# A two-layer hybrid decoder step on one core: another first stage, and a regrouping of function tables, splits and masks on the other engines

## The chip, the core and the metric

The kernel runs on one core of one Trainium2 chip, as one program. The metric is the device time of a run in microseconds; where several runs are given, it is their median. The core's engines are TensorE (PE in the rows), VectorE (DVE), ScalarE (ACT), GpSimd (POOL) and the queue of SyncE (SP); they run at the same time and meet at semaphores. PEld is TensorE's weight load, PEq the sequencer of TensorE.

## The reference

`reference.py` computes one inference step of two layers for a prompt of 512 tokens and eight samples of eight tokens each (576 tokens in all), at a model width of 1024. Layer 0 has Mamba-2 heads and sparse-attention heads in parallel, layer 1 gated DeltaNet heads and dilated sliding-window heads; each layer ends in a squared-ReLU MLP of width 4096, with a root-mean-square norm before and after mixer and MLP. The work starts with

```python
y = x * rsqrt(mean(x * x) + eps) * norm_w
```

for all 576 tokens, and the inputs of the convolutions and of the mixers' step sizes are products of this y.

## The kernel before

Tokens are kept turned: 128 partitions hold 128 of the 1024 channels, one tile for each k from 0 to 7 (KT = 8), with the 576 tokens (TOK) in the free dimension. Every f32 product is made from rounded parts: `HH` is the high part of the activations (fp32r), `HTr` the low part, and of each weight chunk ScalarE writes the high part (`split_high`, L283, the CAST in the rows) and GpSimd the low part (`split_low`, L295); then high x high, high x low and low x high are three matmuls of 288 columns. Chunks of weights are 1 MB and come through a ring of buffers that SyncE's queue fills (`fill_ring`).

The program is a list of stages. Each stage is a block: all engines meet at its end (`L114`), so a stage lasts until its last engine is done. Inside a stage each engine runs its instructions in the order in which they are written; nothing is scheduled by a planner. `split_high(K, act, n)` and `split_low` send all chunks up to n that have not been sent yet, so where they are called decides in which stage and behind what the work is done.

The stages that the change touches, in order of time: `initialise` (GpSimd makes iotas, VectorE the identity and the masks, the queue starts x, two transfers, and the first weights); `first_norm` (TensorE turns x: for each k five transposes, L362; VectorE and ScalarE copy them out by turns, ScalarE squares 128 x 576 per k, L393, VectorE adds the eight squares, L420; a product with ones sums over the partitions, L367; Ln and Exp give the root, L396 and L398; VectorE multiplies, L427, ScalarE rounds, L401, VectorE subtracts, L431; TensorE makes the products for dt and for sconv's first chunk); the SSM convolution (`project_conv`, units u of 128 channels; its products of gates, L904); `ssm_norm`; the compression of sparse attention; `layer_tail`, once a layer (norms with Ln and Exp at L2313 to L2327, the output and MLP products L2407, L446, L2518 and L2420); `gdn_scalars` (gates of the delta rule, and `LevelMasks`, 30 integer operations of VectorE); two `project_conv` stages for the delta rule, each with `roots`, which normalise q and k, L927 and L931; two times two `gdn_pair` stages, each for two heads a and b, whose steps go by counted semaphores (L3236: identity minus the level-0 matrix; L3239 and L3240: k times beta and k times decay); and after each two pairs `gdn_norm`, whose end is

```python
            for i in range(N):
                act.activation(RS[:, i, :], RS[:, i, :], ACT.Exp, scale=-0.5).then_inc(rs_ready, 1)
            split_high(K, act, chunk + 1)
```

The CAST of the next chunk stands behind the norm's functions on ScalarE, and `split_low(K, pool, chunk + 1)` is all that GpSimd has in that stage.
## Time and profile before

| what | value |
|---|---|
| median of 3 runs | 2828.17 us (2827.36 to 2830.39) |
| time of the profiled execution | 2830.34 us |
| span in its trace, first to last instruction | 2827.7 us |
| mean granted clock of TensorE | 0.948 of full speed |
| instructions | 44348 |
| TensorE busy | 2577.0 us, 91% of the span |
| VectorE, ScalarE, GpSimd busy | 1253.7, 966.6, 910.6 us |

The profiled execution took 2.6 us more than its span, and 2.2 us more than the median. All durations below are from it. A row of a timeline is the start, the duration, the engine, the line, the operation, what it writes and reads, and in brackets the idle time before it and what ended it.

### The profile page before, as it was taken

How to read it: one execution, taken by the hardware profiler on the slowest of the kernel's cores; microseconds unless marked ns; L12 is line 12 of the kernel's file. 1: busy time of each engine (PE TensorE's matmuls, PEld its weight loads, DVE VectorE, ACT ScalarE, POOL GpSimd, SP SyncE). 2: the span in 40 equal slices, each digit the busy share in tenths (PEclk: the TensorE clock that was granted, in tenths of full speed). 3: DMA queues.
4: the chain of work that ended last, by engine and by line, in shares of the span. 5: the costliest groups of instructions: out<-in, count | busy, mean ns of one | idle time of the engine just before them, and what ended most of it. 6: DMA issues, size and time to landing. Idle time of an engine off the chain costs nothing. (4 is left out here: it accounts for less than half of the span.)

```text
span 2827.7 us, 44348 instructions
## 1 busy us (share of the span) xinstructions
PE 2577.0 (91%) x18431; PEld 2302.5 (81%) x18431; DVE 1253.7 (44%) x2509; ACT 966.6 (34%) x1743; POOL 910.6 (32%) x449
## 2 busy tenths in 40 slices
PE   7889899987989999989988898889998887999997
PEld 5856796556979999978977797778776687999997
DVE  6785303776152223364644365432126444422225
ACT  4442222663252112152632353231225434221212
POOL 2351230332353333342344234423320015433331
PEclk9989998998999999989998899889999998999999
DMA  5212465330312222222211121112330532222221
GB/s 157 92 40 87 83 134 180 157 161 1 90 60 75 90 75 90 75 79 81 75 33 32 32 75 33 32 32 81 108 116 6 173 116 68 76 89 81 84 88 51
DMA packets 206677, 232.74 MB, mean 82 GB/s; under 512 B 40460, under 2 KB 165228, under 8 KB 205870
## 3 DMA queue, kind: packets, MB, share of 16 engines
q1 hardware_dynamic: 204398, 229.66, 26.0%
...
q10 hardware_dynamic: 2080, 0.25, 0.1%
...
## 5 line engine op out<-in xcount | busy, mean ns | idle before, releaser
L295 POOL TENSOR_TENSOR WRr<-WR,WH 128x2048 fp32r<-128x2048 f32 (+2 forms) x100 | 440.7, 4407 | 1040.9 <-ACT WH L283 949.1
L2407 PE MATMUL PS<-HHr,WRr 128*128 128x288 f32 x1104 | 327.0, 296 | 0.0
L283 ACT CAST WH<-WR 128x2048 fp32r<-128x2048 f32 (+2 forms) x100 | 182.2, 1823 | 355.1 <-DMA WR<-in_mlp_w 140.8
L446 PE MATMUL PS<-YTr,WRr 128*128 128x288 f32 x1024 | 303.5, 296 | 0.0
L446 PE MATMUL PS<-HHr,WH 128*128 128x288 f32 (+1 forms) x896 | 271.9, 303 | 22.4 <-PEq L114 21.0
L446 PE MATMUL PS<-YTr,lt_WX 128*128 128x288 f32 x1408 | 282.1, 295 | 0.0
L446 PE MATMUL PS<-HTr,WH 128*128 128x288 f32 (+1 forms) x896 | 268.8, 300 | 0.0
L446 PE MATMUL PS<-HHr,WRr 128*128 128x288 f32 (+1 forms) x896 | 268.6, 300 | 0.0
L295 POOL TENSOR_TENSOR WRr<-WR,lt_WX 128x2048 fp32r<-128x2048 f32 x34 | 157.9, 4645 | 256.4 <-ACT lt_WX L283 256.4
L2407 PE MATMUL PS<-HHr,WH 128*128 128x288 f32 x800 | 237.5, 297 | 0.3 <-POOL WRr L295 0.3
L2407 PE MATMUL PS<-HTr,WH 128*128 128x288 f32 x800 | 237.0, 296 | 0.0
L446 PEld LDWEIGHTS PS<-YTr,lt_WX 128*128 128x128 f32 x1408 | 227.3, 188 | 0.1
L2407 PEld LDWEIGHTS PS<-HHr,WRr 128*128 128x128 f32 x1104 | 209.1, 189 | 0.0
L446 PEld LDWEIGHTS PS<-YTr,WRr 128*128 128x128 f32 x1024 | 192.1, 188 | 0.0
L446 PEld LDWEIGHTS PS<-HHr,WH 128*128 128x128 f32 (+1 forms) x896 | 171.7, 192 | 24.6 <-POOL WRr L295 16.4
L2819 DVE TENSOR_TENSOR YT<-YT 128x576 f32<-128x576 f32 x64 | 55.0, 860 | 276.6 <-ACT YT L2711 265.9
L446 PEld LDWEIGHTS PS<-HTr,WH 128*128 128x128 f32 (+1 forms) x896 | 171.7, 192 | 0.6
L446 PEld LDWEIGHTS PS<-HHr,WRr 128*128 128x128 f32 (+1 forms) x896 | 171.4, 191 | 0.6
L476 PE MATMUL PS<-WH,HHr 128*128 128x512 f32 (+2 forms) x400 | 154.8, 387 | 6.1 <-PEq L114 6.1
L476 PE MATMUL PS<-WRr,HHr 128*128 128x512 f32 (+3 forms) x400 | 152.9, 382 | 0.0
L2711 ACT ACTIVATE YT<-PS 128x576 f32<-128x576 f32 x56 | 36.5, 652 | 340.3 <-PE PS L2407 340.3
L2407 PEld LDWEIGHTS PS<-HHr,WH 128*128 128x128 f32 x800 | 151.3, 189 | 0.7 <-POOL WRr L295 0.6
...
## 6 DMA issues: line engine op xcount, KB each, us to landing
...
```

Source lines behind the costliest of these rows:

```text
L283: act.copy(high_slot(K, i, used), K.WR[:, n % RING, 0:used]).then_inc(K.hi, 1)
L295: pool.tensor_tensor(K.WRr[:, n % RING, 0:used], K.WR[:, n % RING, 0:used], high_slot(K, i, used).bitcast(F32), ALU.subtract).then_inc(K.l ...
L446: last = pe.matmul(out, a, b, start=(n == 0), stop=(n == 3 * len(terms) - 1))
L476: last = pe.matmul(K.PS[0:a.shape[1], bank, 0:n], a, w[:, k, :], start=(half == 0 and k == 0 and m == 0), stop=(half == 1 and k == kt - 1 ...
L2407: last = pe.matmul(out, a[:, k, c], h[:, k, x], start=(n == 0), stop=(n == 3 * KT - 1))
L2711: act.activation(in_halves(whole(r, j)), both_halves(K, u % 2), ACT.Relu).then_inc(relu_done, 1)
L2819: dve.tensor_tensor(x, x, x, ALU.mult).then_inc(sq_done, 1)
```

## The change

The stage `initialise` is dissolved into `first_norm`. x comes in five transfers, one per tile of 128 tokens; TensorE turns a tile as it lands; ScalarE sums the squares of each tile token by token, with the accumulator, so the root is one number per partition; a diagonal matrix of the roots (`DG_`) is the moving operand of a second product of x, which comes out turned and scaled in one; ScalarE multiplies by the norm's weight and rounds to `HHr`, VectorE makes `HTr` in one operation. The dt products stand between the scaled ones, the sconv products behind them all. The masks are made between the copies of tiles.

Beside that: `logs_and_exps` puts one table set that has both Ln and Exp in front of the norms, `roots` and both layer tails, and four further stages load a named set at their start; with it the program has 33 table loads, before 62. In the SSM convolution the products and functions of the gates' sums stand two units later. `LevelMasks` moves from `gdn_scalars` into the first `project_conv` of the delta rule, four operations a unit. The split of chunk + 2 in `gdn_scalars` stands ahead of a wait. In `gdn_pair` the order of VectorE's L3236 and L3239/L3240 changes, and the last pair takes over the split of chunk + 1, which `gdn_norm` had.

```diff
+def logs_and_exps(act):
+    act.preload_act_table_set("natural_log_exp_and_others")
...
+                for t, n in TILES:
+                    src = K.x_prompt[0][t * P:(t + 1) * P, :] if t < NT else K.x_sample.rearrange("b s d -> (b s) d")
+                    sp.dma_start(XS[0:n, t, :], src).then_inc(K.x_tile[t], 16)
+                fill_ring(K, sp, RING - 1)
...
+                logs_and_exps(act)
+                act.wait_ge(x_zero, 3)
+                for t, n in TILES:
+                    act.wait_ge(K.x_tile[t], 16)
+                    if t:
+                        act.wait_ge(sq_done, t)
+                    act.activation(SQ[0:n, :], XS[0:n, t, :], ACT.Square, accum_out=ss[0:n, t:t + 1]).then_inc(sq_done, 1)
+                inv_rms(act, K, ss[:], D, sq_done, TT, rs_link).then_inc(rs_done, 1)
+                act.wait_ge(rs_done, 1)
+                act.wait_ge(ident_in, 1)
+                for t in range(TT):
+                    act.mul(DG_[:, t, :], K.ident[:], ss[:, t:t + 1]).then_inc(diagonal, 1)
+                split_high(K, act, K.at["dt"])
+                act.wait_ge(small_out, 1)
+                for k in range(KT):
+                    act.wait_ge(h_mm, k + 1)
+                    act.mul(K.HH[:, k, 0:TOK], scaled_x(k), K.normT[:, 0, k:k + 1]).then_inc(hi_done, 1)
+                    if k == 2:
+                        split_high(K, act, K.at["sconv"])
...
+                pe.wait_ge(x_copied, TT)
                 for k in range(KT):
-                    if k % 2:
-                        act.wait_ge(turned, k + 1)
-                        act.copy(K.XT[:, k, 0:TOK], K.PSF[:, (k % 3) * 1024:(k % 3) * 1024 + TOK]).then_inc(x_act, 1)
-                    x_copied(act, k)
                     if k >= 2:
-                        act.wait_ge(added, k - 1)
-                    act.activation(SQ[:, k % 2, :], K.XT[:, k, 0:TOK], ACT.Square).then_inc(sq_done, 1)
-                split_high(K, act, K.at["sconv"])
-                act.wait_ge(summed, 1)
-                act.activation(in_halves(RS[:]), K.PS[:, 6:8, 0:HALF], ACT.Ln, scale=1.0 / D, bias=K.eps[:]).then_inc(rs_link, 1)
-                act.wait_ge(rs_link, 1)
-                act.activation(RS[:], RS[:], ACT.Exp, scale=-0.5).then_inc(rs_done, 1)
+                        pe.wait_ge(hi_done, k - 1)
+                        pe.wait_ge(lo_done, k - 1)
+                    for t, n in TILES:
+                        if k == 0:
+                            pe.wait_ge(diagonal, t + 1)
+                        last = pe.matmul(scaled_x(k)[:, t * P:t * P + n], XS[0:n, t, k * P:(k + 1) * P], DG_[0:n, t, 0:n],
+                                         start=True, stop=True)
+                    last.then_inc(h_mm, 1)
...
+                    if k == 1:
+                        dt_w = split_wait(K, pe, K.at["dt"])
+                        pe.wait_ge(small_out, 2)
+                    if k >= 1:
+                        dense(k - 1, dt_w, SH, 6)
+                dense(KT - 1, dt_w, SH, 6).then_inc(K.mm, 1)
+                conv_w = split_wait(K, pe, K.at["sconv"])
                 for k in range(KT):
-                    act.wait_ge(h_done, k + 1)
-                    act.copy(K.HH[:, k, 0:TOK], K.HT[:, k, 0:TOK]).then_inc(hi_done, 1)
-                act.wait_ge(heads_in, 48)
-                act.activation(rowp[:, 0, :], rowp[:, 0, :], ACT.Exp)
+                    last = dense(k, conv_w, P, 0)
+                last.then_inc(K.mm, 1)
...
+                for k in range(KT):
+                    dve.wait_ge(hi_done, k + 1)
+                    dve.scalar_tensor_tensor(K.HTr[:, k, 0:TOK], scaled_x(k), K.normT[:, 0, k:k + 1],
+                                             K.HH[:, k, 0:TOK].bitcast(F32), ALU.mult, ALU.subtract).then_inc(lo_done, 1)
...
-                        dve.scalar_tensor_tensor(K.HT[:, k, 0:TOK], K.XT[:, k, 0:TOK], K.normT[:, 0, k:k + 1], RS[:],
-                                                 ALU.mult, ALU.mult).then_inc(h_done, 1)
-                    if k >= 1:
-                        dve.wait_ge(hi_done, k)
-                        dve.tensor_tensor(K.HTr[:, k - 1, 0:TOK], K.HT[:, k - 1, 0:TOK], K.HH[:, k - 1, 0:TOK].bitcast(F32),
-                                          ALU.subtract).then_inc(lo_done, 1)
...
@@ -729,16 +732,18 @@
         pool.iota(self.pi[:], [[0, P]], base=0, channel_multiplier=1).then_inc(self.drawn, 1)
-    def build(self, K, dve):
-        do = Chain(dve, self.link)
+    def begin(self, dve):
+        self.do = Chain(dve, self.link)
         dve.wait_ge(self.drawn, 3)
-        do(dve.tensor_tensor(self.xr[:], self.fi[:], self.pi[:], ALU.bitwise_xor))
-        do(dve.tensor_scalar(self.lo[:], self.diff[:], 1024, None, ALU.is_gt))
-        for k in range(7):
-            do(dve.tensor_scalar(self.t1[:], self.xr[:], 1 << k, None, ALU.is_ge))
-            do(dve.tensor_scalar(self.t2[:], self.xr[:], 2 << k, None, ALU.is_lt))
-            do(dve.tensor_tensor(self.t1[:], self.t1[:], self.t2[:], ALU.mult))
-            do(dve.tensor_tensor(K.LV[:, k, :], self.t1[:], self.lo[:], ALU.mult))
+        self.do(dve.tensor_tensor(self.xr[:], self.fi[:], self.pi[:], ALU.bitwise_xor))
+        self.do(dve.tensor_scalar(self.lo[:], self.diff[:], 1024, None, ALU.is_gt))
+    def level(self, K, dve, k):
+        do = self.do
+        do(dve.tensor_scalar(self.t1[:], self.xr[:], 1 << k, None, ALU.is_ge))
+        do(dve.tensor_scalar(self.t2[:], self.xr[:], 2 << k, None, ALU.is_lt))
+        do(dve.tensor_tensor(self.t1[:], self.t1[:], self.t2[:], ALU.mult))
+        do(dve.tensor_tensor(K.LV[:, k, :], self.t1[:], self.lo[:], ALU.mult))
 class DilatedMasks:
@@ -898,7 +905,7 @@
                     pe.matmul(K.PS[:, 7, 0:TS], K.ones[:], qk.RS[:, i, SEQ:TOK], start=True, stop=True).then_inc(summed, 1)
-                if c and u == 4:
+                if c and u == 6:
                     pe.wait_ge(cum_in, 1)
@@ -922,6 +929,7 @@
         def roots(act, i0):
+            logs_and_exps(act)
             for i in (i0, i0 + 2):
@@ -962,7 +970,7 @@
                     act.activation(c.sm[0][:], c.sm[0][:], ACT.Exp, scale=-1.0).then_inc(exp_out, 1)
-                if c and u == 6:
+                if c and u == 8:
                     act.wait_ge(cum_out, 1)
@@ -988,6 +996,10 @@
             for u in range(n_ch):
+                if levels and u == 1:
+                    levels.begin(dve)
+                if levels and 1 <= u <= LEVELS:
+                    levels.level(K, dve, u - 1)
                 if c and u == 1:
@@ -1548,6 +1560,7 @@
             def _(act):
+                act.preload_act_table(ACT.Silu)
                 for i, (c, t) in enumerate(units):
@@ -1598,6 +1611,7 @@
                               allow_slow_non_contiguous=True).then_inc(nw_in, 16)
+                logs_and_exps(act)
                 for t in range(TT):
@@ -1762,10 +1776,14 @@
                 act.activation(HSr[:, kv, :], K.PS[0:R, 2 + kv, 0:QW], ACT.Silu).then_inc(hid_silu, 1)
+            act.preload_act_table(ACT.Silu)
             hidden(0)
+            act.preload_act_table(ACT.Exp)
             act.wait_ge(s_ready, 1)
             act.activation(flat, flat, ACT.Exp, scale=SCALE).then_inc(exp_done, 1)
+            act.preload_act_table(ACT.Silu)
             hidden(1)
+            act.preload_act_table(ACT.Exp)
         @block.tensor
@@ -2638,6 +2656,7 @@
             def _(act):
+                logs_and_exps(act)
                 k0 = 0
@@ -2948,7 +2967,6 @@
                 pool.memset(BAT[:, TOK:TP], 0.0).then_inc(padded, 1)
-                masks.draw(pool)
                 split_low(K, pool, chunk + 2)
@@ -2957,6 +2975,7 @@
                 act.dma_start(C.nw[:], K.gdn_norm_w[0].unsqueeze(1), allow_slow_non_contiguous=True).then_inc(rows_in, 16)
+                act.preload_act_table(ACT.Sigmoid)
                 act.wait_ge(K.mm, K.end[chunk])
@@ -2966,10 +2985,10 @@
                 act.activation(sm[0][:], sm[0][:], ACT.Exp, scale=-1.0).then_inc(exp_out, 1)
+                split_high(K, act, chunk + 2)
                 act.wait_ge(cum_out, 1)
...
                 act.activation(eg[:], gcf, ACT.Exp).then_inc(exp_out, 1)
-                split_high(K, act, chunk + 2)
             @block.tensor
@@ -2996,7 +3015,6 @@
             def _(dve):
-                masks.build(K, dve)
                 do = Chain(dve, dve_link)
@@ -3051,6 +3069,7 @@
         def _(act):
+            logs_and_exps(act)
             for i in range(N):
@@ -3118,7 +3137,7 @@
                  + ["VT", "VN4", "O"])
-    dve_steps = (["DT", "LT1", "LT", "QKD", "TT0", "tok"]
+    dve_steps = (["DT", "LT1", "LT", "QKD", "tok", "TT0"]
                  + [x for k in KS for x in ([("TM", k), ("TT", k)] if k < LEVELS - 1 else [("TT", k)])]
@@ -3163,7 +3182,7 @@
             if last_pair:
-                split_low(K, pool, chunk)
+                split_low(K, pool, chunk + 1)
             if not last_pair:
@@ -3198,6 +3219,8 @@
                     act.copy(tile_(b.TM, t), tile_(b.A, t)).then_inc(acts[a], 1)
+            if last_pair:
+                split_high(K, act, chunk + 1)
             o = 1536
@@ -3232,12 +3255,11 @@
             for a, b in enumerate(B):
-                dve.wait_ge(pools[a], PO["L0"])
-                dve.tensor_tensor(t5(b.TT), bc(K.ident[:], 1, TT), t5(b.TT), ALU.subtract).then_inc(dves[a], 1)
-            for a, b in enumerate(B):
                 dve.wait_ge(pes[a], PE["ktok"])
...
                 dve.tensor_tensor(t5(b.kdec), t5(b.A), bc(C.dl[:, :, b.h], 2, P), ALU.mult).then_inc(dves[a], 1)
+                dve.wait_ge(pools[a], PO["L0"])
+                dve.tensor_tensor(t5(b.TT), bc(K.ident[:], 1, TT), t5(b.TT), ALU.subtract).then_inc(dves[a], 1)
             for k in KS:
@@ -3299,7 +3321,7 @@
             for a, b in enumerate(B):
-                pe.wait_ge(dves[a], DV["tok"])
+                pe.wait_ge(dves[a], DV["TT0"])
                 turn(b.A, b.TT).then_inc(pes[a], 1)
```

ScalarE at the delta-rule norm of the first two pairs; `L3057` and `L3062` are Ln and Exp of the root, `L283` is the CAST of the weight chunk. Before:

```order
L3052 UNCONDITIONAL_BRANCH
L3055 ACTIVATE YT<-g_SX 128x576 x4
L3057 ACT_TABLE_LOAD
L3057 ACTIVATE YT<-PS,eps 128x4x512
L3058 ACTIVATE YT<-PS,eps 128x4x64
L3062 ACT_TABLE_LOAD
L3062 ACTIVATE YT<-YT 128x576 x4
L283 CAST WH<-WR 128x2048
```

After, where the same functions are at L3076 and L3081, and `L311` is `logs_and_exps`:

```order
L3070 UNCONDITIONAL_BRANCH
L311 ACT_TABLE_LOAD
L3074 ACTIVATE YT<-g_SX 128x576 x4
L3076 ACTIVATE YT<-PS,eps 128x4x512
L3077 ACTIVATE YT<-PS,eps 128x4x64
L3081 ACTIVATE YT<-YT 128x576 x4
L114 UNCONDITIONAL_BRANCH
```

Of the two loads one is left, and it stands ahead of the squares; the CAST has left the stage.

VectorE in a pair, where `YT` holds the first head's matrix, `k_big` the second's. Before:

```order
L3233 TENSOR_TENSOR YT<-PS,YT 128x640
L3233 TENSOR_TENSOR k_big<-PS,k_big 128x640
L3236 TENSOR_TENSOR YT<-ident,YT 128x640
L3236 TENSOR_TENSOR k_big<-ident,k_big 128x640
L3239 TENSOR_TENSOR X<-PS,g_beg 128x640
L3240 TENSOR_TENSOR g_SX<-PS,g_dl 128x640
L3239 TENSOR_TENSOR X<-PS,g_beg 128x640
L3240 TENSOR_TENSOR g_SX<-PS,g_dl 128x640
```

After (L3262 is the operation of L3236):

```order
L3256 TENSOR_TENSOR YT<-PS,YT 128x640
L3256 TENSOR_TENSOR k_big<-PS,k_big 128x640
L3259 TENSOR_TENSOR X<-PS,g_beg 128x640
L3260 TENSOR_TENSOR g_SX<-PS,g_dl 128x640
L3262 TENSOR_TENSOR YT<-ident,YT 128x640
L3259 TENSOR_TENSOR X<-PS,g_beg 128x640
L3260 TENSOR_TENSOR g_SX<-PS,g_dl 128x640
L3262 TENSOR_TENSOR k_big<-ident,k_big 128x640
```

The first head's two products with gates stand ahead of both subtractions, the second head's between them.

TensorE at the start of the program after the change; L418 turns x, L421 and `L830` turn the small rows, L444 is x by the diagonal (for k = 0 and 1), L432 the dt products:

```order
L418 MATMUL PS<-ident,YT 128x128 x32
L418 MATMUL PS<-ident,YT 128x64 x8
L421 MATMUL PS<-ident,YT 128x64
L830 MATMUL PS<-ident,YT 128x29 x12
L444 MATMUL PS<-YT 128x128 x4
L444 MATMUL PS<-YT 128x64
L444 MATMUL PS<-YT 128x128 x4
L444 MATMUL PS<-YT 128x64
L432 MATMUL PS<-HHr,WH 16x288
L432 MATMUL PS<-HTr,WH 16x288
```

The eight transposes of each tile follow one another and precede the small rows, which came first before; 40 products of L444 are new, 24 dt products come six at a time behind them.

## Rows read from the trace of the kernel before

**Rows 1.** The page: busy us, share of the span and instructions of each engine.

```profile
PE 2577.0 (91%) x18431; PEld 2302.5 (81%) x18431; DVE 1253.7 (44%) x2509; ACT 966.6 (34%) x1743; POOL 910.6 (32%) x449
```

**Rows 2.** Waits of PE by line: us in total, times, longest us.

```profile
PE PS L446 <- PEq L114: 21.0, 6, 6.4
...
PE PS L3284 <- DVE g_SX L3240: 17.8, 7, 4.0
...
PE PS L2420 <- ACT HHr L2386: 12.0, 3, 4.6
...
PE PS L3274 <- PEq L114: 11.5, 4, 3.6
...
PE PS L904 <- DVE s_la L1000: 1.5, 1, 1.5
```

**Rows 3.** Timeline of ACT, POOL, PE, delta-rule norm: start, us, idle before.

```profile
1599.85 1.28 ACT L3062 ACT_TABLE_LOAD   x1
1601.14 2.41 ACT L3062 ACTIVATE YT<-YT 128x576 f32<-128x576 f32 x4
1603.45 1.88 ACT L283 CAST WH<-WR 128x2048 fp32r<-128x2048 f32 x1
...
1605.41 4.49 POOL L295 TENSOR_TENSOR WRr<-WR,WH 128x2048 fp32r<-128x2048 f32 x1 [37.51 <-ACTq L114]
...
1610.26 0.58 PE L446 MATMUL PS<-HHr,WH 128*128 128x288 f32 x1 [6.39 <-PEq L114]
```

**Rows 4.** Windows: length, busy of each engine, PEclk, DMA share, GB/s.

```profile
1610.20:1613.60 3.40, 3.34 (x14) 3.37 (x15) 2.06 (x7) 0.87 (x4) 0.80 (x3) 0.50 0.02 5
```

**Rows 5.** The chain that ended last, by time: start, us, what.

```profile
2402.37 1.28 ACT L2315
...
2411.36 35.69 PE PS L2407 x267
...
2808.85 1.28 ACT L2315
```

**Rows 6.** Timeline of PE, DVE and ACT in the first stage.

```profile
13.61 10.79 PE L362 MATMUL PS<-ident,YT 128*128 128x128 f32 x40
...
37.20 0.82 DVE L427 SCALAR_TENSOR_TENSOR HT<-X,normT,fn_rs 128x576 f32<-128x576 f32 x1
...
49.39 0.63 ACT L936 COPY s_DTT<-PS 16x576 f32<-16x576 f32 x1 [6.34 <-PEq L114]
```

**Rows 7.** Groups of ACT by line and form: squares with a sum.

```profile
L1604 ACT ACTIVATE n_sq<-YT 128x1024 f32<-128x1024 f32 x5 | 5.3, 1060 | 1.6 <-PEq L114 1.4
```

**Rows 8.** Timeline of PE, DVE and POOL in the first delta-rule pair.

```profile
1428.81 1.28 PE L3279 MATMUL PS<-g_SX 128*128 128x128 f32 x10
...
1434.80 1.82 DVE L3236 TENSOR_TENSOR YT<-ident,YT 128x640 f32<-128x640 f32 x1
1436.54 2.15 DVE L3236 TENSOR_TENSOR k_big<-ident,k_big 128x640 f32<-128x640 f32 x1
1438.61 0.81 DVE L3239 TENSOR_TENSOR X<-PS,g_beg 128x640 f32<-128x640 f32 x1
...
1435.89 2.11 POOL L3156 TENSOR_TENSOR k_big<-k_big,LV 128x640 f32<-128x640 f32 x1
...
1440.21 0.77 PE L3284 MATMUL PS<-ident,YT 128*128 128x128 f32 x5 [4.01 <-DVE g_SX L3240]
1441.67 1.33 PE L3284 MATMUL PS<-ident,k_big 128*128 128x128 f32 x5 [0.70 <-DVE g_SX L3240]
```

**Rows 9.** Timeline of ACT: end of a conv stage, start of a tail.

```profile
1411.88 1.28 ACT L931 ACT_TABLE_LOAD   x1
...
2290.35 4.68 ACT L2645 CAST lt_AH<-YT 128x576 fp32r<-128x576 f32 x8 [4.09 <-PEq L114]
```

**Rows 10.** Timeline of POOL and PE at the end of `gdn_scalars`.

```profile
1325.16 4.52 POOL L295 TENSOR_TENSOR WRr<-WR,WH 128x2048 fp32r<-128x2048 f32 x1 [19.60 <-ACT WH L283]
...
1330.03 0.37 PE L446 MATMUL PS<-HHr,WH 128*128 128x288 f32 x1 [3.04 <-PEq L114]
```

253 lines of the change are left out of this document (119 added, 134 removed).

## The prediction

> **What bounds the kernel now.** I read the page first: TensorE is busy for 2577.0 us of a span of 2827.7 [rows 1], so the other engines matter only where TensorE waits for them. The waits of TensorE by line say where that is [rows 2]: 21.0 us in six waits of L446 for "PEq L114", which is the barrier at a stage's end; 11.5 in four such waits of L3274; 17.8 at L3284 in the delta-rule pairs; 12.0 at L2420 in the layer tails and 1.5 at L904. A barrier names no culprit, so for each I read the timeline of all engines just before it and looked for the engine that finished last. The edit list is long, so the sum below is a list of such places.
>
> **1. The end of the delta-rule norm (the largest term).** ScalarE's table load, its exponentials, then a CAST of 1.88 us from 1603.45, then GpSimd's low half of 4.49 us from 1605.41, and only then the barrier; TensorE has stood 6.39 us when it starts at 1610.26, so it was done at 1603.9 [rows 3]. The change takes the CAST and the low half out of this stage and puts them behind the VN copies of the last pair. It also takes the load at 1599.85 out of the chain. ScalarE then ends its exponentials at about 1599.85 + 2.41 = 1602.3, before TensorE at 1603.9, so the stage ends with TensorE's last product and the wait shrinks to about 0.4 of barrier: 6.0 saved, twice (two passes), 12.0. Bounds: if the moved CAST or GpSimd step delays the last pair by its 1.88 or 4.49 less what is idle there, 4.0 each, 8.0 in all; 12.8 if the barrier vanishes too. I take 12.0, since GpSimd had been idle 37.51 us before that step. The load now put at this stage's start stands before squares that TensorE's sums use only after half a projection product: hidden; without that cover 1.28 each.
>
> **2. The clock after that pause.** In the window behind it the granted clock is 0.50 and 14 matmuls take 3.34 us, 0.24 each [rows 4]; in a long undisturbed piece of the chain 267 take 35.69, 0.134 each [rows 5]. A clock of 0.50 is the level of 1.2 GHz, 1.00 that of 2.4. So 14 x 0.106 = 1.5 is lost there, and somewhat more until the clock is whole. With a pause of 0.4 I expect none of it: 1.75 each, 3.5 in all (0 to 4).
>
> **3. The first stage.** Now TensorE turns x from 13.61 to 24.4 (40 turns of 0.27) after all of x has landed and after a barrier; VectorE then needs two operations per k, the first 0.82, before TensorE has its operands; ScalarE's first row of the next stage is at 49.39, so the last product was at 49.1 [rows 6]. After the change five smaller transfers bring x, turns start with the first of them and end about 15. Squares are five of 1.06 [rows 7], some 6 us from the second tile on, in step with arrival, so the root and the diagonals are there at about 16.5. Then come 40 added products of f32, x by diagonal. The nearest row is L3279: five such take 1.28 us at full clock [rows 8]. With six dt products at 0.134 a k takes 1.28 + 0.8 = 2.1, more than ScalarE's or VectorE's one operation per k (0.7 and 0.8), so TensorE sets the pace. At half clock a k is 3.7; I count two such. From 16.5: 2 x 3.7 + 6 x 2.1 = 20.0, so 36.5, and 48 products for sconv at 0.134, 6.4: 42.9 against 49.1. Saved 6.2; I take 6.5, since dt products of the first k may fill its waits. Bounds: 4 (clock low for one k more and x late by 1) to 8 (no low k but one). The masks of `initialise` lie between VectorE's copies of tiles, which TensorE's waits for x cover. Uncovered they would cost about 1 us.
>
> **4. The delta-rule pairs.** TensorE waits 4.0 at L3284 at 1440.21, and VectorE's rows say why: two operations L3236 of 1.82 and 2.15, held by GpSimd's 2.11 beside them, stand ahead of the four of 0.81 that TensorE waits for [rows 8]. The change puts the first head's two ahead of its L3236, and TensorE's turn now waits for that head's L3236. The three operations, 0.75 + 0.75 + 1.8 behind 1434.8, end at 1438.1, so the first turn comes some 2 us sooner. But the product that follows (the first head's X) queues behind the second head's turn, now at 1441.67, and that waits for three more operations, 0.75 + 0.75 + (0.8 free or 2.15 held): 1440.4 to 1441.7. So 0 to 1.3 a pair; I take 0.9, nearer the free value, since by then GpSimd's row has ended: 3.6 in four (0 to 5.2).
>
> **5. Table loads.** Each is 1.28. Exp and Ln are now in one set, and 62 loads in the program become 33, but only those on the path pay. *Layer tails*: on the chain that ended last stand the loads at 2402.37 and 2808.85 [rows 5], and the wait of L2420, 12.0 in three [rows 2], holds one each. Of the three places with L2420 each saves one load in full, and a little of a second that GpSimd's low halves mostly absorb: 1.6, 1.5, 1.6; the last norm of the program saves 1.3. Together 6.0 (4.5 to 7). *Against it*: at each of the two tails' starts a load now stands in front of the CAST at 2290.35, which stands first behind a barrier and feeds TensorE's first product [rows 9]: minus 2.6 (minus 2.6 to 0). *Scaling by roots in the conv stages*: the load at 1411.88 lies on ScalarE's unbroken chain to the barrier of L3274's wait [rows 2, 9]: 1.28 twice, 2.6. *The SSM norm* has two loads ahead of the scaling for which TensorE waits, and keeps none there but brings one in front of its squares: 1.3 net. *Compression*: 0.3.
>
> The load at 1599.85 ends at 1601.13, and the exponentials that it serves, 2.41 long, start at 1601.14: no time is lost behind a load [rows 3]. The Trainium skill ("ScalarE: Activation LUTs", What ACT_TABLE_LOAD costs) gives a switch as 1283 ns and a further drain of about 1380, 2.66 us together; by it the net seven exposed loads would be worth some 10 us more.
>
> **6. Gates of the delta rule (`gdn_scalars`).** GpSimd's low half, 4.52 from 1325.16, is the last work before a barrier after which TensorE's first row, at 1330.03, has waited 3.04 [rows 10]: TensorE was done at 1327.0. Moved ahead of a wait the low half ends over 10 us earlier, and the stage ends with TensorE: 2.7, and 0.6 of TensorE's wait for the gates, since VectorE no longer builds masks ahead of them: 3.3. Bounds: 0 if GpSimd now holds VectorE's chain of gates for its 4.5; 4.5 if the gates come forward wholly. The masks' 30 short VectorE operations go into the following conv stage, four a unit in seven units. From the 0.82 of 576 columns [rows 6] I estimate 0.3 each for 128, so 1.2 a unit, hidden by VectorE's waits for TensorE there; uncovered up to 8.
>
> **7. The SSM conv stage.** The product L904 waits 1.5 for s_la [rows 2]; two units later it no longer does: 1.4 (0 to 1.4).
>
> **Sum**: 12.0 + 3.5 + 6.5 + 3.6 + 6.0 - 2.6 + 2.6 + 1.3 + 0.3 + 3.3 + 1.4 = 37.9. The profiled execution took 2830.3, the median of the runs is 2828.2. From the one 2792.4, from the other 2790.3; I forecast 2792, nearer the first, whose durations these are.
>
> **Rivals.**
> *The moved steps take back what they gave.* The low half in the last pair holds VectorE's operations there, the pair order only exchanges one held operation for another, and the gates' chain is held by GpSimd. For it: L3236 takes 1.82 and 2.15 where its like take 0.81, beside GpSimd's 2.11 [rows 8]. Against: GpSimd's idle 37.51 [rows 3]. Then the norm gives 8.0, pairs 0, gates 0, clock 2: 20 to 25 saved, 2806. Chance 0.25.
> *Loads cost more than their row.* By the price of 1.28 nine exposed loads go and two come; were about as much again lost behind each, the net seven times 1.3 is some 9 us: 2783. Against: the rows at 1599.85 and 1601.14 [rows 3]. Chance 0.06. The page of the Trainium skill named above has this rule.
> *The change does little*: barriers are ended by something I misread (a transfer that lands late) in most places. The six waits of L446 stay, 2825. Chance 0.04.
> *Slower, by the clock.* TensorE's 2577.0 busy us scale with the granted clock, 0.948 on average in this execution, and a pause lowers it for some time after [rows 4]. If other, newly cut pauses (the interleaved first stage, tails that start with a load) lowered the mean by 1.5 points, 37.9 would be gone (37.9/2577 = 0.0147); at 1.7 points it is slower by over 0.2%: 2834. Against: the change shortens pauses nearly everywhere. Chance 0.03.
>
> **How the numbers follow.** 0.62 for the forecast (30 to 46 saved). The ends of all terms together give 17 to 47 saved, 2811 to 2781; to hold eight in ten, with the rival of loads and most of that of moved steps in it, I give 2780 to 2808. 0.2% is 5.7 us, about what can be told from no change; faster by more than that: 0.62 + 0.25 + 0.06 = 0.93, same 0.04, slower 0.03.
>
> **What would show it.** TensorE's first L446 after the delta-rule norm waits under 1 us instead of 6.39, and the window behind has a clock near 1.00; the first stage's products end near 43; L3284's longest wait falls to about 3; TensorE's first product at a tail's start waits 1.3 more; no load stands between Ln and Exp in the tails; L446 behind `gdn_scalars` waits under 1 instead of 3.04. The prediction is wrong if the last pair grows by what the norm loses, if L3284's wait is the same, or if products of x by the diagonal take over 2 us per k at full clock.

## The result and the profile after

The changed kernel takes 2793.39 us, the median of four runs (2791.05 to 2795.49), against 2829.28 before on the same chips: a ratio of 0.9872 (95% interval 0.9855 to 0.9889), 36 us less. The forecast was 2792. Its profiled execution took 2795.49 with a span of 2793.7, 34.0 less than before, at a mean granted clock of 0.952.

The page's row of TensorE's busy time, then its waits by line (total, times, longest); they answer to [rows 1] and [rows 2]:

```profile
PE 2574.2 (92%) x18507; PEld 2303.9 (82%) x18507; DVE 1256.8 (45%) x2494; ACT 928.3 (33%) x1717; POOL 910.6 (33%) x450
...
PE PS L2323 <- POOL lt_SS L2384: 14.5, 5, 5.5
PE PS L3296 <- PEq L114: 11.0, 4, 3.6
PE PS L3306 <- DVE YT L3262: 7.8, 4, 2.0
PE PS L535 <- PEq L114: 6.7, 6, 2.1
...
PE PS L3306 <- DVE k_big L3262: 5.7, 4, 1.4
PE PS L2438 <- ACT HHr L2404: 6.3, 3, 2.1
...
PE PS L535 <- POOL WRr L295: 3.1, 2, 3.0
PE PS L2536 <- DVE YTr L2803: 7.1, 2, 3.6
```

TensorE's busy time is that of before within 3 us, so nearly all that was gained is waiting. The six barriers of L446 (now L535) cost 6.7 instead of 21.0, L2420 (L2438) 6.3 instead of 12.0, L3284 (L3306) 7.8 + 5.7 instead of 17.8. The four barriers of L3274 (L3296) hardly moved, 11.0 instead of 11.5, and some waits grew, two of them on lines that the change touches: L2518 (L2536) at the tails' starts from 4.5 to 7.1, and a new one of 3.0 for GpSimd at L535.

A sum of waits doesn't say where time went, so I cut each trace at TensorE's first row behind each barrier with a wait. The lengths between such rows are the measure of all that follows (us, worked out from the starts of these rows; the last ends with the span):

| stretch | before | after | change |
|---|---|---|---|
| first stage and SSM convolution | 133.34 | 127.12 | -6.22 |
| SSM products | 131.52 | 131.04 | -0.48 |
| SSM gate | 47.44 | 48.11 | +0.67 |
| SSM norm | 23.70 | 22.60 | -1.10 |
| sparse attention up to the selection | 306.78 | 307.20 | +0.42 |
| selection and first layer tail | 656.16 | 653.08 | -3.08 |
| gates of the delta rule | 31.09 | 28.43 | -2.66 |
| first delta-rule convolution | 91.34 | 91.77 | +0.43 |
| pairs 1 and 2 | 167.11 | 162.09 | -5.02 |
| first delta-rule norm | 21.78 | 15.74 | -6.04 |
| second delta-rule convolution | 96.78 | 93.28 | -3.50 |
| pairs 3 and 4 | 165.12 | 162.60 | -2.52 |
| second delta-rule norm | 23.15 | 16.38 | -6.77 |
| projections behind it | 45.79 | 47.07 | +1.28 |
| dilated attention, without its last part | 279.48 | 279.98 | +0.50 |
| its last part and second tail, to the end | 607.12 | 607.21 | +0.09 |

The largest term is seen in the timeline (start, us, engine, what, idle before) and a window (length, busy by engine, PEclk, DMA share, GB/s) of the changed kernel; they answer to [rows 3] and [rows 4]:

```profile
1571.41 1.28 ACT L311 ACT_TABLE_LOAD   x1 [8.09 <-PEq L114]
1582.87 2.41 ACT L3081 ACTIVATE YT<-YT 128x576 f32<-128x576 f32 x4
...
1587.18 0.37 PE L535 MATMUL PS<-HHr,WH 128*128 128x288 f32 x1 [0.30 <-PEq L114]
...
1587.10:1602.00 14.90, 14.82 (x112) 14.85 (x113) 10.82 (x26) 8.34 (x18) 5.42 (x4) 1.00 0.22 71
```

ScalarE's exponentials follow Ln without a load and end at 1585.3, TensorE's last product starts at 1586.6 and ends at 1586.9, and its wait is 0.30 instead of 6.39; behind it 112 matmuls begin in 14.9 us at a clock of 1.00, 0.133 each.

The first stage, which answers to [rows 6]:

```profile
14.18 0.30 ACT L317 ACTIVATE fn_ss<-fn_ss,eps 128x5 f32<-128x5 f32 x1
14.75 0.40 ACT L399 ACTIVATE YT<-ident,fn_ss 128x128 f32<-128x128 f32 x1
...
15.30 5.28 PE L444 MATMUL PS<-YT 128*128 128x128 f32 x20 [1.35 <-ACT YT L399]
28.11 1.41 PE L444 MATMUL PS<-YT 128*128 128x128 f32 x10
...
43.23 0.63 ACT L944 COPY s_DTT<-PS 16x576 f32<-16x576 f32 x1 [8.53 <-PEq L114]
```

The root is there at 14.7, and the first diagonal (L399) follows. The first two k take 5.28 for 20 records of L444 at a granted clock of 0.50, later ones 1.41 for ten, and ScalarE's first row of the next stage stands at 43.23 instead of 49.39.

### The profile page after: what moved, and what is told of

It is laid out like the page before. It is cut to its first block and busy times, and to the rows that moved or that the text cites. A ratio compares the mean times of both kernels' runs of the same rounds, so it can differ in the third digit from the quotient of the medians.

```text
span 2793.7 us, 44441 instructions
## 1 busy us (share of the span) xinstructions
PE 2574.2 (92%) x18507; PEld 2303.9 (82%) x18507; DVE 1256.8 (45%) x2494; ACT 928.3 (33%) x1717; POOL 910.6 (33%) x450
## 5 line engine op out<-in xcount | busy, mean ns | idle before, releaser
L535 PE MATMUL PS<-YTr,WRr 128*128 128x288 f32 x1024 | 303.5, 296 | 0.0
L283 ACT CAST WH<-WR 128x2048 fp32r<-128x2048 f32 (+2 forms) x100 | 182.4, 1824 | 343.2 <-DMA WR<-in_mlp_w 141.1
L535 PE MATMUL PS<-YTr,lt_WX 128*128 128x288 f32 x1408 | 282.1, 295 | 0.0
L535 PE MATMUL PS<-HHr,WH 128*128 128x288 f32 (+1 forms) x896 | 270.4, 302 | 12.4 <-PEq L114 6.7
L535 PE MATMUL PS<-HTr,WH 128*128 128x288 f32 (+1 forms) x896 | 267.3, 298 | 0.0
L535 PE MATMUL PS<-HHr,WRr 128*128 128x288 f32 (+1 forms) x896 | 267.1, 298 | 0.0
L535 PEld LDWEIGHTS PS<-YTr,lt_WX 128*128 128x128 f32 x1408 | 227.3, 188 | 0.1
L535 PEld LDWEIGHTS PS<-YTr,WRr 128*128 128x128 f32 x1024 | 192.1, 188 | 0.0
L535 PEld LDWEIGHTS PS<-HHr,WH 128*128 128x128 f32 (+1 forms) x896 | 170.2, 190 | 15.0 <-issue 8.0
L535 PEld LDWEIGHTS PS<-HTr,WH 128*128 128x128 f32 (+1 forms) x896 | 170.1, 190 | 0.6
L535 PEld LDWEIGHTS PS<-HHr,WRr 128*128 128x128 f32 (+1 forms) x896 | 169.9, 190 | 0.6
L2853 DVE TENSOR_TENSOR lt_AHf<-lt_AHf,PS 128x576 f32<-128x576 f32 x88 | 66.4, 755 | 190.8 <-PE PS L535 190.8
```

The source lines that it names most:

```text
L283: act.copy(high_slot(K, i, used), K.WR[:, n % RING, 0:used]).then_inc(K.hi, 1)
L535: last = pe.matmul(out, a, b, start=(n == 0), stop=(n == 3 * len(terms) - 1))
L2853: dve.tensor_tensor(acc, acc, ps, ALU.add).then_inc(acc_done, 1)
```

## The experiments

Each kernel has one profiled execution, whose stretches I compare, and times beside the kernel before on the same chip. The first four start from the kernel before and add one part of the change.

One trace per kernel has its own spread, and it is not small beside the effects. Among the kernels with the new first stage, stretches whose code they share differ: the SSM convolution, from ScalarE's first row on, takes 82.34 to 83.91 us, the first delta-rule norm 15.74 to 17.12, the third pair 77.91 to 80.94. In all three the lengths go with the granted clock. So a difference of 1 to 3 us in one stretch counts here only where a wait in the rows explains it.

**e1, the norm's tail alone.** `split_high` and `split_low` of the next chunk leave `gdn_norm`:

```diff
                 act.activation(RS[:, i, :], RS[:, i, :], ACT.Exp, scale=-0.5).then_inc(rs_ready, 1)
-            split_high(K, act, chunk + 1)
...
             if last_pair:
-                split_low(K, pool, chunk)
+                split_low(K, pool, chunk + 1)
...
+            if last_pair:
+                split_high(K, act, chunk + 1)
```

> The kernel before, with one part of the change: the split of the next chunk leaves the delta-rule norm and stands behind the VN copies of the last pair. My theory (GpSimd's low half ended the norm's stage, and the pause cooled TensorE's clock): TensorE's wait behind the norm falls from 6.4 to under 1.6 in both passes, one table load still being in ScalarE's chain (its exponentials then end at about 1603.5, before TensorE at 1603.9), so 12 us go with the waits and 1 to 3 more with the clock: 13 to 15 saved, and the last pairs keep their lengths within 0.5. Rival (the moved steps take back): the last pairs grow by 2 to 4 each and only 4 to 8 are saved.

2817.78 against 2828.9, ratio 0.9957 (0.9940 to 0.9974): 11.1 saved, less than the 13 to 15 expected. The norms are 16.53 and 17.88 long instead of 21.78 and 23.15, so 5.3 saved in each, with waits of 1.1; the convolution behind the first is 2.10 shorter, the last pairs keep their lengths (84.81 and 84.85 against 84.83 and 84.27). But the projections behind the second norm are 1.53 longer. So the first pass's last pair keeps its length to 0.02 and the second's is 0.58 longer, far from the 2 to 4 of the rival: the moved steps take nothing back that can be told from the spread. The clock's gain comes once and not twice.

**e2, the shared table set alone**, in the SSM norm, `roots`, the tails and `gdn_norm`:

```diff
         def roots(act, i0):
+            logs_and_exps(act)
```

> The kernel before, with only the shared table set for Ln and Exp (delta-rule norm, roots, SSM norm, layer tails). Theory by rows: a load is worth 1.28 where ScalarE's chain ends the wait. SSM norm 1.1, norm of the delta rule 1.3 twice, inside the tails 2.4 + 1.4 and 1.3 + 1.9 and 1.3 at the end, against 1.3 at each of two tail starts; roots 0 to 0.4, since SyncE's stores end that stage. Sum about 9 saved (7 to 11). Rival (a load costs 2.66 with a drain): 16 to 20 saved, and gaps of 1.3 behind the removed loads vanish with them. Rival (roots on the path as I predicted): 2.2 more, with the wait behind the conv stages at 2.4 instead of 3.6.

2810.82 against 2828.9, ratio 0.9933 (0.9916 to 0.9949): 18.1 saved, twice what I expected. The stretches: convolutions of the delta rule -1.44 and -1.55, the pairs behind them -1.85 and -1.80, SSM norm -1.10, first tail -3.26, second norm -1.47, projections behind it -1.18, last stretch -6.94; the first stretch is 1.26 longer. In the tails the rows say how (start, us, idle before). TensorE's first product of the second tail in e2:

```profile
2279.95 0.58 PE L2525 MATMUL PS<-lt_AH,WH 128*128 128x288 f32 x1 [3.61 <-DVE YTr L2792]
```

ScalarE's loads and the product behind them in the first tail of the kernel before, and that product in e2:

```profile
803.47 1.28 ACT L2324 ACT_TABLE_LOAD   x1
...
805.65 1.28 ACT L2327 ACT_TABLE_LOAD   x1
...
808.50 0.58 PE L2420 MATMUL PS<-HHr,lt_WX 128*128 128x288 f32 x1 [4.61 <-ACT HHr L2386]
```

```profile
808.38 0.58 PE L2427 MATMUL PS<-HHr,lt_WX 128*128 128x288 f32 x1 [2.10 <-ACT HHr L2393]
```

The product behind ScalarE's CAST waits 2.10 in all three places, where it waited 4.61, 3.38 and 3.98. The rows of the kernel before tell how many loads that is. At the first place both stand in the open, behind the CAST of the weights: 2.51 less, for two loads. At the second, ScalarE waits 2.71 for TensorE behind the first load, so only the second load (at 1234.93) counts: 1.28 less. At the third there are two again (2381.37 and 2383.55), but TensorE still works beside most of the first: 1.88 less. One load more goes from TensorE's wait for GpSimd ahead of it (the load at 2367.57; 6.73 to 5.46), one at the program's end (7.69 to 6.41), and the load ahead of the CASTs costs 1.3 (3.61 against 2.33).

The Trainium skill ("ScalarE: Activation LUTs", What ACT_TABLE_LOAD costs) gives 2.66 us a switch, with a drain of 1.38 in it, and the total of e2 lies where the rival with a drain had it. The traces don't agree with that rule: these waits fall by about 1.3 for each load in the open, and no row shows a drain; in the changed kernel Exp at 1582.87 starts when Ln, at 1582.38 with 0.46, ends, and before, the load's 1.28 lay between the two and nothing more (1599.85 to 1601.14). What is beyond my sum lies elsewhere. The waits of the tails fall by 7.2 net, where I had 5.7. The convolutions give 3.0 where I had 0 to 0.4; a wait of 0.96 at L899 went in each. The pairs, which have none of the loads removed, give 3.65, with a higher granted clock in their first 8.9 us (0.81 instead of 0.65 in the first, 1.00 instead of 0.81 in the third). And the last part of attention, which has none removed either, took 69.25 instead of 71.38 with the new load taken off. The last two, nearly 6 us, no load pays for in any row.

**e3, the first stage alone.**

> The kernel before, with only the first stage of the change. Theory: ScalarE's first row of the conv stage at 43.2 instead of 49.4, as in the changed kernel, and the SSM conv stage keeps its length, so 6 us saved at 133 us of the span and also at the end (5 to 7), unless a stage that is set by transfers takes some of it back. Rival (the conv stage is set by weights that land at fixed times): half of it is gone at 133.

2824.01 against 2828.9, ratio 0.9983 (0.9973 to 0.9992), ten runs. At TensorE's row behind the SSM convolution 5.9 are saved, as expected. The median has 4.9 of it; in the trace the last part of attention, up to the tail's first product, is 74.46 long instead of 71.38. That stretch comes up under e9.

**e4, VectorE's order in the pairs alone.**

```diff
             for a, b in enumerate(B):
-                dve.wait_ge(pools[a], PO["L0"])
-                dve.tensor_tensor(t5(b.TT), bc(K.ident[:], 1, TT), t5(b.TT), ALU.subtract).then_inc(dves[a], 1)
-            for a, b in enumerate(B):
                 dve.wait_ge(pes[a], PE["ktok"])
...
+                dve.wait_ge(pools[a], PO["L0"])
+                dve.tensor_tensor(t5(b.TT), bc(K.ident[:], 1, TT), t5(b.TT), ALU.subtract).then_inc(dves[a], 1)
```

> The kernel before, with only VectorE's order in the delta-rule pairs. Theory: the wait of 4.0 at L3284 becomes 2.0 + 1.4, the stage 1.2 to 1.4 shorter, four times: 5 saved (4 to 6). In the changed kernel the first two pairs were 2.5 shorter; if that was the order alone, and not a clock that was higher for other reasons, they are 2.5 shorter here too and 7 to 8 are saved.

2821.42 against 2828.9, ratio 0.9975 (0.9964 to 0.9986): 7.5 saved by the medians, above the 4 to 6 of the first forecast. The pairs are 1.50, 2.31, 1.24 and 1.16 shorter, 6.2 together; the first two, with 3.8, are short of the 5 that the second forecast wanted from the order alone. The changed kernel's rows of VectorE and TensorE, which answer to [rows 8]:

```profile
1421.43 0.81 DVE L3259 TENSOR_TENSOR X<-PS,g_beg 128x640 f32<-128x640 f32 x1
1422.16 0.81 DVE L3260 TENSOR_TENSOR g_SX<-PS,g_dl 128x640 f32<-128x640 f32 x1
1422.89 1.85 DVE L3262 TENSOR_TENSOR YT<-ident,YT 128x640 f32<-128x640 f32 x1
1424.66 0.81 DVE L3259 TENSOR_TENSOR X<-PS,g_beg 128x640 f32<-128x640 f32 x1
...
1426.13 0.81 DVE L3262 TENSOR_TENSOR k_big<-ident,k_big 128x640 f32<-128x640 f32 x1
...
1424.80 0.76 PE L3306 MATMUL PS<-ident,YT 128*128 128x128 f32 x5 [1.97 <-DVE YT L3262]
1426.99 0.76 PE L3306 MATMUL PS<-ident,k_big 128*128 128x128 f32 x5 [1.43 <-DVE k_big L3262]
```

The first head's L3262 is still held (1.85), the second's is free (0.81), and TensorE's two waits are 1.97 and 1.43 instead of 4.01 and 0.70: 1.3 less, 5.2 in four pairs. What the second pair has beyond that was there before its waits, with a clock of 0.80 instead of 0.67 in its first 8.9 us.

The next kernels start from the changed kernel and alter one thing. The intervals of e5 to e9 and of e11 all overlap with the changed kernel's (0.9855 to 0.9889), so their totals don't part them from it for certain; what is said of them rests on waits in their traces.

**e5, the tails' table load behind the first CASTs.**

```diff
             def _(act):
-                logs_and_exps(act)
                 k0 = 0
...
                     k0 += kt
+                logs_and_exps(act)
```

> The changed kernel, with the table load of the layer tails behind the first CASTs and copies instead of ahead of them. Theory (the load stands on the chain to TensorE's first product): TensorE's wait at a tail's start falls from 3.5 and 3.6 to 2.2 and 2.3, 2.6 us saved against the changed kernel, nothing lost later, since ScalarE is idle there. Rival (ring or activations set the start): no change.

2790.31, ratio to before 0.9864 (0.9845 to 0.9883; the changed kernel's is 0.9872). TensorE's first product of each tail and its wait:

```profile
688.25 0.58 PE L2536 MATMUL PS<-lt_AH,WH 128*128 128x288 f32 x1 [2.17 <-DVE YTr L2803]
...
2260.06 0.58 PE L2536 MATMUL PS<-lt_AH,WH 128*128 128x288 f32 x1 [2.33 <-DVE YTr L2803]
```

2.17 and 2.33, as before the change, instead of 3.46 and 3.61. The last stretch is 2.45 shorter, though 1.5 of the gain lies in the part of attention ahead of the tail, which the edit doesn't touch; the first tail's stretch is 653.08 in both. So the theory holds for the waits; that their 2.6 us are gained in the total is not shown.

**e6, the stores ahead of the refill, two of six through ScalarE's queue.**

```diff
-            fill_ring(K, sp, last_chunk + RING)
+            fill_ring(K, sp, last_chunk + RING - (1 if qk else 0))
             sp.wait_ge(kept_out, 3)
-            store_conv_state(K, sp, rows, out_p, out_s, cols)
+            store_conv_state(K, sp, rows, out_p, out_s, cols[0:2] if qk else cols)
+            fill_ring(K, sp, last_chunk + RING)
```

> The changed kernel; in both delta-rule conv stages four of the six stores of the conv state go before the last refill of the ring, and two of them through ScalarE's queue. Theory (SyncE's six issues behind TensorE's last product end the stage, at 1408.8): the wait behind the stage falls from 3.2 and 3.6 to about 2.0, 1 to 1.3 less in each, 2.3 saved. Rival (ScalarE's chain, as the prediction had it): ScalarE ends later by its own two issues, so the wait is unchanged or 0.5 longer.

2786.98, ratio 0.9859 (0.9841 to 0.9877). SyncE's queue in the changed kernel at the end of the first delta-rule convolution, with TensorE's next row, and then that row of e6:

```profile
1406.59 0.46 SPq L1063 DMA_DIRECT2D out_gdn_conv_p<-X  x1
...
1408.51 0.30 SPq L1064 DMA_DIRECT2D out_gdn_conv_s<-X  x1
...
1409.35 1.10 PE L3296 MATMUL PS<-YT,ones 128*128 128x512 f32 x2 [3.21 <-PEq L114]
```

```profile
1405.66 1.10 PE L3299 MATMUL PS<-YT,ones 128*128 128x512 f32 x2 [1.90 <-PEq L114]
```

In the changed kernel six stores go out one after another from 1406.59, behind a refill that waits for TensorE's last product, and the barrier falls when the last is issued; ScalarE had ended at 1406.8. With the stores ahead TensorE waits 1.90 instead of 3.21, in the second stage 1.66 instead of 3.57. That shows what ends the stage in the changed kernel. In the kernel before it was in part ScalarE after all; its copies and the first store there read

```profile
1417.30 1.51 ACT L975 COPY X<-PS 27x512 f32<-27x512 f32 x3
...
1418.84 0.28 SPq L1051 DMA_DIRECT2D out_gdn_conv_p<-X  x1
```

The refill had been issued by 1418.13, and the first store waited 0.7 more for ScalarE's copies, which stand behind the roots and end at 1418.81. So of the 1.28 of a load only some 0.7 lay on the way to that barrier; with the load gone the first store follows the refill at once, in e2 as well (1414.45 behind 1414.40).

The first pair behind each stage is shorter too, by 1.60 and 2.57, and the first window of the pair goes with it (the row of the changed kernel, then that of e6):

```profile
1409.30:1419.30 10.00, 9.63 (x46) 6.60 (x47) 6.29 (x8) 3.94 (x5) 1.39 (x1) 0.83 0.62 179
```

```profile
1405.60:1415.60 10.00, 9.63 (x61) 7.55 (x62) 7.53 (x10) 3.94 (x5) 3.03 (x2) 1.00 0.78 212
```

The clock is 0.83 behind the pause of 3.21 and 1.00 behind that of 1.90. That the shorter pause is the reason is not shown: the third pair had a clock of 1.00 in its first 8.9 us also behind 3.25 in e5, where it is 1.58 shorter than in the changed kernel with no edit near it, and e10 has 0.83 behind 1.90.

**e7, the roots' load put back** (the call removed from `roots`).

> The changed kernel, with a table load again between Ln and Exp in the roots of the delta rule's conv stages. The prediction's step (load on the chain to the barrier): the wait behind the two stages grows by 1.28 each, 2.6 slower. Theory now (SyncE's stores end the stage, 1.9 behind ScalarE): 0 to 0.3 each.

2799.20, ratio 0.9895 (0.9877 to 0.9914): 6 slower than the changed kernel by the medians, and neither number of the two on record: the convolutions are 3.32 and 1.30 longer (and the gates' stage, not touched, 1.5). My theory of the stores is right on the stage's end (e6) and was wrong on the loads. TensorE's waits in the middle of the first of these stages, in the changed kernel and in e7:

```profile
PE PS L906 <- ACT g_RS L961: 1.4, 1, 1.4
```

```profile
PE PS L906 <- ACT g_RS L960: 2.8, 1, 2.8
```

`roots` is called twice in a stage. The first call stands in front of ScalarE's copies of the next units, and TensorE's sum of squares (L906, before L899) waits for them: 1.36 with one load, 2.80 with two. In the 10 us behind that row the clock is 0.84 instead of 1.00, and 56 matmuls begin instead of 67, 1.5 us; the barrier's wait is 0.40 longer. These three make up the 3.32. In the second stage a wait of 0.96 stands at L906 where there was none. So a load is worth 1.0 to 1.4 in the middle of the stage, as much again where the pause lowers the clock, and little at the barrier.

**e8, an earlier CAST in the SSM convolution.**

```diff
+                if c and u % 2 == 1:
+                    split_high(K, act, first + u // 2 + 2)
                 if u >= 1:
                     silu(act, u - 1)
```

> The changed kernel; in the SSM conv stage ScalarE's CAST of the next chunk stands ahead of the silu that waits for VectorE. Theory (the gates' wait of 1.45 was replaced by one of 2.95 for GpSimd's low half, whose CAST queues behind that silu): the wait of 2.95 at L535 goes, 2 to 3 us saved at the end of that stage. Rival (VectorE's chain bounds the stage): TensorE waits elsewhere in the stage as long, and nothing is saved.

2787.30, ratio 0.9846 (0.9822 to 0.9871). The wait of 2.95 at L535 is gone and the first stretch is 123.31 instead of 127.12, 3.8 less. The rows of the changed kernel, ScalarE, GpSimd and TensorE:

```profile
71.70 0.69 ACT L929 ACTIVATE s_SX<-YT 128x576 f32<-128x576 f32 x1 [7.12 <-DVE YT L1041]
72.29 1.90 ACT L283 CAST WH<-WR 128x2048 fp32r<-128x2048 f32 x1
...
74.27 5.01 POOL L295 TENSOR_TENSOR WRr<-WR,WH 128x2048 fp32r<-128x2048 f32 x1 [11.76 <-ACT WH L283]
...
79.33 0.59 PE L535 MATMUL PS<-HHr,WH 128*128 128x288 f32 x1 [2.95 <-POOL WRr L295]
```

The silu at 71.70 waited 7.12 for VectorE, the CAST queued behind it, and GpSimd's low half behind the CAST. From ScalarE's first row on, the stage takes 79.50 in e8, and again in e10 and e12, which have the same edit; it takes 83.87 to 83.91 in the changed kernel, e5, e7 and e11, and 82.34 and 82.36 in e6 and e9, which have the wait as well. So 2.9 is the wait. The other 1.5 is the clock behind it, and that isn't the same each time: the window from 70 to 85 of the changed kernel and of e6, whose code and wait are the same there, read

```profile
70.00:85.00 15.00, 12.05 (x82) 11.82 (x80) 15.00 (x31) 6.89 (x13) 5.01 (x1) 0.89 0.23 71
```

```profile
70.00:85.00 15.00, 12.05 (x94) 11.82 (x93) 15.00 (x32) 7.19 (x13) 5.79 (x2) 1.00 0.22 71
```

**e9, TensorE's stream shifted by 16 instructions** (the turn of the norm's rows made 17 times).

> The changed kernel with 16 turns of the small rows repeated in the first stage, where TensorE waits anyway, so that every later TensorE instruction sits 16 places further in its stream. In the changed kernel the last stage of attention, with the caches' transfers, was 3.7 us longer than before beyond the 1.3 of the table load, with TensorE idle for 'issue' at five places. Theory (the stalls hang on where in its stream TensorE has to fetch while the transfers run): from the stage's first row to the tail's first product another value than 76.3, by over 1.5 either way, and the issue gaps at other rows. Rival (they hang on the other engines' earlier arrival): 76.3 within 0.5 and gaps at the same rows.

2798.22 in two runs, ratio 0.9890 (0.9872 to 0.9908). From the first row of the last part of attention to the tail's first product it took 80.24. Four of TensorE's five rows idle for "issue" in the changed kernel, then the longest waits of that kind in e9:

```profile
2216.48 0.38 PE L3799 MATMUL PS<-ident,d_V 128*64 128x128 f32 x2 [0.53 <-issue]
...
2224.13 0.33 PE L3796 MATMUL PS<-ident,d_V 128*128 128x128 f32 x1 [0.69 <-issue]
...
2231.77 0.49 PE L3796 MATMUL PS<-ident,d_V 128*128 128x128 f32 x3 [0.72 <-issue]
...
2239.70 0.38 PE L3772 MATMUL PS<-ident,HH 128*128 128x128 f32 x2 [0.96 <-issue]
```

```profile
PE PS L3815 <- issue: 5.1, 2, 3.3
```

The same stretch, before the tails' load, in all kernels: 71.4, 71.1 and 71.0 in before, e1 and e4, and 69.3 in e2, though e1, e2 and e4 reach it up to 11 us earlier; 74.5 in e3, whose TensorE stream is shifted by the new first stage and nothing else; 71.4 to 75.5 in the other kernels with that stage; 79.0 in e9 (1.28 taken off where the load is in front). Both parts of the theory's forecast came: another length, and gaps at another line. That the place in the stream is the cause is not shown by it: with one and the same stream of TensorE the stretch still spreads by 4 us, e9 is one trace, and its 79.0 is 3.5 above the longest of the others. The gaps are also only part of it. They add up to 1.2 us before, 3.5 in the changed kernel and 5.4 in e9, and the granted clock of the stretch falls with them, 0.92, 0.90 and 0.86.

The repeated turns did something that I hadn't asked for. They fill TensorE's time ahead of the first products with the diagonal, its wait there is 0.39 instead of 1.35, and its row of the first two k is

```profile
15.18 3.09 PE L445 MATMUL PS<-YT 128*128 128x128 f32 x20 [0.39 <-ACT YT L399]
```

3.09 where the changed kernel has 5.28; from 15 to 22 us the clock is 1.00 instead of 0.55. ScalarE's first row of the convolution stands at 41.08 instead of 43.23. In one trace, 16 turns of 0.06 us each, whose result nobody needs, bought 2.15.

**e11, the level masks back in the stage of the gates**, ahead of the gates, all else as changed.

> The changed kernel with the level masks back in the stage of the gates, ahead of the gates on VectorE, while the split of the second chunk stays ahead of the wait. Theory (the masks, held by GpSimd's splits, slowed the first delta-rule conv stage by 1.9, and the stage of the gates owes its 2.7 to the split's place alone): gates 28.4 to 29.5, conv stage 89.9 instead of 91.8, 1 to 2 us faster in all. Rival (the prediction: masks are hidden in the conv stage and delay the gates): conv stage unchanged, gates' stage 1 to 4 longer.

2800.24, ratio 0.9895 (0.9880 to 0.9910), 7 slower than the changed kernel by the medians. The convolution is 90.11 instead of 91.77 and has no wait in its middle, as I expected. A row of VectorE in the changed kernel shows what the masks do there:

```profile
1366.12 5.09 DVE L1038 SCALAR_TENSOR_TENSOR YT<-YT,g_HW 128x512 f32<-128x512 f32 x1
```

The masks' operations are 0.22 to 0.29 each, but they push VectorE's own work under GpSimd's split, which starts at 1365.89 with 4.77: three of these operations take 5.08 or 5.09 there instead of 0.74. In e11 the splits meet VectorE's waits more often, and the three longest such rows are 3.93, 2.65 and 2.34.

But the gates' stage is 35.08 instead of 28.43, outside both forecasts. Its rows of GpSimd, VectorE and TensorE:

```profile
1291.83 4.61 POOL L295 TENSOR_TENSOR WRr<-WR,WH 128x2048 fp32r<-128x2048 f32 x1 [0.97 <-ACT WH L283]
...
1292.01 4.58 DVE L745 TENSOR_TENSOR l_t<-l_t 128x128 int32<-128x128 int32 x1
...
1306.58 4.55 POOL L295 TENSOR_TENSOR WRr<-WR,WH 128x2048 fp32r<-128x2048 f32 x1 [10.14 <-ACT WH L283]
...
1306.72 4.45 DVE L1097 TENSOR_SCALAR h_sm<-h_sm 128x40 f32<-128x40 f32 x1
...
1314.87 0.38 PE L3012 MATMUL PS<-g_g,UN 128*128 128x8 f32 x1 [5.89 <-DVE g_g L3032]
```

Each of GpSimd's two splits holds one operation of VectorE for its length: the first a mask operation (4.58 instead of 0.29), the second one on 40 columns (4.45 instead of 0.18), and TensorE waits 5.89 for the gates instead of 1.2. The changed kernel has the second of these holds too, at 1301.30 with 4.48; the kernel before has the first, at 1301.13 with 4.58, and its second split behind the gates. Only e11 has both. The other 2 us of the stage are clock: TensorE's rows from the gates on take 10.0 at 0.63 instead of 8.1 at 0.79. So the split may stand ahead of the gates only if the masks leave. The other half, masks out and the split left where it was, was not run.

**e10 and e12, the best of these together.** e10 is the changed kernel with e5, e6 and e8 and without the load at the start of the SSM gate; e12 has the masks back as well.

> The changed kernel with the late table load in the tails, the stores ahead of the refill, the early CAST in the SSM conv stage, and without the load at the start of the SSM gate. If the gains add up: 1.3 (one tail at least) to 2.6, 2.5 for the stores and 2 to 4 for the pairs behind them with a higher clock, 3 to 4 for the SSM conv stage, 0.7 for the gate: 10 us under the changed kernel, 2780 to 2785. If they only exchange waits: within 4 us of it.

> The kernel of e10 with the level masks back in the stage of the gates. Theory as for e11: 1 to 2 us faster than e10. Rival: slower by 1 to 4.

e10 takes 2782.10, ratio 0.9820 (0.9799 to 0.9840) to before, against the changed kernel's 0.9872 (0.9855 to 0.9889): 11 us less by the medians, as expected, and the intervals are apart. Its five runs lie between 2771.92 and 2785.20. e12 takes 2785.06, ratio 0.9827 (0.9807 to 0.9847), which the intervals don't part from e10; its gates' stage is 7.1 longer, its first convolution 2.3 shorter, and the theory of 1 to 2 us faster did not come.

## Why the prediction was right, and where it was not

The total was right to 1.4 us of the median, by terms that erred in both directions, and that it is so near is luck. In the traces 34.0 us were saved, and 37.9 was the sum. Pairs and tails gave 7 more than forecast; the clock, the roots, the SSM convolution and the gates gave about 6 less, and the last part of attention, in no term, lost 3.7. The steps, by their numbers:

1. *Delta-rule norm*, 12.0 forecast: 6.04 and 6.77, 12.8, and e1 shows it alone with 5.3 each, the load making up the rest. The mechanism held to the row: waits of 0.30, ScalarE done before TensorE. The first norm takes up to 17.12 in other kernels with this stage, so another trace of the same edit could have shown 1.4 less.
2. *Clock behind it*, 3.5 forecast: about 2 behind the first norm (3.50 less the 1.55 of the loads), and nothing behind the second, where the stretch grew by 1.28 (1.53 in e1). There TensorE waits for an X of VectorE that comes 25.1 us after the start either way (25.4 before): it waits 2.58 instead of 1.39, and the clock from there to the stage's end is 0.92 instead of 1.00. The step that failed took each place as limited by TensorE.
3. *First stage*, 6.5 forecast: 6.16 at its end (43.23 against 49.39), by the sum's own course: a clock of 0.50 for the first two k, 2.15 per k later. Two k at the low clock took 6.4 with the dt products of one, where the sum had 7.4, and the start was at 15.3 and not at 16.5; one late wait of 0.88 took part of that back. In e3 the last part of attention is 3.1 longer, and the median has 4.9 and not 5.9; whether the 76 more TensorE records of the first stage are the reason stays open (e9). The low clock of the first k, which the sum took as given, was not: e9 is without it.
4. *Pairs*, 3.6 forecast, at most 5.2: 6.2 alone (e4), 7.5 in the changed kernel. The mechanism was right and the term sized too low: the second head's L3262 ran free each time, which brings 1.3 a pair, the top of the bounds. What goes beyond 5.2 is clock, which the term had at nothing.
5. *Table loads*. Tails 6.0 less 2.6 forecast, 3.4: 3.1 net in the first stretch, 4.9 behind the first product of the second (535.74 to 530.88), less the 1.3 ahead of it, so 6.7. The step that failed is "each saves one load in full, and a little of a second": at the first place two loads stood in the open and the wait fell by 2.51, at the third by 1.88, and a load ahead of them was on the path too (6.73 to 5.46). The load in front of the CAST costs what was said (e5). Roots 2.6 forecast: 1.44 and 1.55 (e2), the size near, and the place mostly wrong: "ScalarE's unbroken chain to the barrier" held the stores before that barrier for some 0.7 of the load's 1.28 and no more, the stores themselves end the stage (e6), and most of the gain lies in the middle of it (e7). In the changed kernel the masks took the first stage's part back. SSM norm 1.3: 1.10. Compression 0.3: nothing seen.
6. *Gates*, 3.3 forecast: 2.66, of which 2.2 is the barrier's wait (3.04 to 0.86). The gates themselves end 20.1 us after the stage's start instead of 20.6: the bound "if GpSimd now holds VectorE's chain of gates for its 4.5" came true (4.48 at 1301.30), and the masks that left had been held as long (4.58 at 1301.13). "Hidden by VectorE's waits", said of the masks in the convolution, failed: they are as short as estimated but bring VectorE's other operations under GpSimd's splits, and the stage was 1.9 longer than with the tables alone (91.77 against 89.90 in e2). But with the split moved and the masks left in place, the gates' stage would be 6.7 longer (e11).
7. *SSM convolution*, 1.4 forecast: nothing (83.95 before, 83.89 after, from ScalarE's first row on). The wait of 1.45 was only the first of two; behind it stood 2.95 for a CAST that queues behind VectorE's chain (e8).

Not in the sum at all: 0.67 lost in the SSM gate, where the load put in front of a CAST makes GpSimd's low half late by 0.38. In e8 and e10 the CAST of that chunk is already done in the stage before, and the stage takes 47.43 and 47.46 (47.44 before), in e8 with the load still at its start.

Of the rivals, the moved steps took nothing back in the pair (e1), but the moved masks did in the first delta-rule convolution (e11). That loads cost more than their row was not borne out: each on a path was worth 1.3 to 1.4 in a wait, and more of them were on paths than the sum had (e2, e7). The slower rival's mechanism, pauses that lower the clock, was seen in both directions, but the mean clock rose from 0.948 to 0.952.
